# Second block: values token-major first, query/key jobs head by head with attention steps of other heads between their matmuls, output sums taken head by head

## The chip, the cores and the metric

One core of one Trainium2 chip runs the whole program. The metric is the device time in microseconds (us) of one execution, median of the runs.

## What is computed

A model of four layers on 512 tokens of 1024 features, all in float32. The change lies in the second layer (`layer` 1 in the code), whose mixer is differential attention. Of the reference, cut to that:

```
u = x * (1.0 + sc1) + sh1
q, k, v = split(u @ w_in, 3)            # 8 heads, of each two halves c of 64 query/key columns, 128 value columns
logits = einsum('bhcqd,bhckd->bhcqk', q * 64 ** -0.5, k) + bias[h]   # keys of later 64-token chunks masked
p = softmax(logits)
pdiff = p[:, :, 0] - lam_full * p[:, :, 1]
out = einsum('bhqk,bhkd->bhqd', pdiff, v)
out = rms_norm_of_each_head(out) * norm_g * (1.0 - lambda_init)
x = layer_norm(alpha * x + (1.0 + g1) * (out @ w_out))
```

Layer 0 (another mixer, and the same gated FFN with a causal convolution) runs before it; an FFN and two more layers follow. The scales, shifts and gates (sc1, sh1, g1, ...) come from a vector c times `w_ada`, 192 tiles in all.

## The kernel before

The activations are kept feature-major: a tile is 128 features by 512 tokens. A product with a weight matrix is a row of **jobs**. A job is one 128-column slice of the weights, all k tiles of it: SP loads 512 KB into `RAW` (two buffers, the load of job j waits for the splitting of job j-2), ACT rounds it to fp32r (`WH`, four slots, waits until PE is through with job j-4), POOL subtracts to get the rest (`WL`, L449), and PE makes three products for each k tile, `WH` by `Uh`, `WH` by `Ul`, `WL` by `Uh` (L1135, L1137 when the bank is part of `junk`), so 24 matmuls of 512 columns for a job of 8 k tiles. Four PSUM banks (0, 1, 4, 7) take the results in turn. Phases of jobs stand in `plan()`; every engine walks through them in this order, in program order.

Beside the jobs run the **ada tiles**: a phase with `ada=a` also has one tile of `w_ada` for each job, from number a on. SP loads it (512 KB), DVE multiplies it by `CB` and sums along the row (`ada_sum`, L1217). Tiles 96 and later need two such sums, for two vectors (L1213 into `junk`, L1214); these are the tiles of double width. In a phase, DVE does the ada tile of a job ahead of the job's epilogue.

Layer 0 ends with `down` of group 2: 8 jobs of only 6 k tiles, 18 matmuls each. Its epilogue is DVE's: `XT` plus bank times gate (L1319), and the running sum of `XT` in `ZS` (L1303) for the layer norm. The ada tiles are 104 to 115 in the phase before it, and none in this phase. The layer norm follows; its last part makes the 8 tiles of `Uh` and `Ul` one by one. POOL scales `XT` in the meantime (L436).

Layer 1's mixer then has these parts:
- `qkcopy`, 16 jobs: eight query tiles, then eight key tiles, copied by ACT to `QD`. Ada tiles 116 to 131.
- `v`, 8 jobs: each is copied to `TT`, transposed on PE by four matmuls (L1101), and copied to `VD` (token-major). Ada tiles 132 to 139.
- Attention in 32 **steps** (head h = it // 4, query tile b = it % 4, keys 0 to 128 (b + 1)). PE: `scores` (L965), two matmuls, one for each half c. DVE: `logits`, scale and bias out of PSUM (L1556), row maximum (L1561). ACT: `diff_exp` (L540). DVE: `diff`, reciprocal, scaling, difference of the two halves (L1571 to L1573) into `PD`. PE: `turn`, transposes of `PD` (L975). ACT: copy to `PTD` (L863). PE: `av`, by the values (L984). ACT: copy to `ON` and squares (L547, L548). PE runs scores two steps ahead of turn. No job runs in this part.
- After all steps: one root (L869), 32 scalings on DVE (L1588), and for each head four transposes (L916), DVE's scaling by `norm_g` (L1595), ACT's rounding to `OH` (L872), DVE's rest to `OL` (L1598).
- `res`, 8 jobs on `OH`, `OL`; then a layer norm.

Of the kernel before, what the change touches and what calls it, by code (L numbers as in the profile page):

```python
# [21 lines left out]
F32 = mybir.dt.float32  # L22
# [32 lines left out]
def plan():  # L55
# [75 lines left out]
def ada_width(a):  # L131

    return 2 if 96 <= a < 164 else 1
# [57 lines left out]
def build(nc, a, out):  # L191
    with ExitStack() as stack:
# [31 lines left out]
        Ul = at("Ul", [KT, TC], A_U + 24 * KB, F32R)  # L224
        ZS = at("ZS", [TC], A_U)
# [48 lines left out]
        DTMP = at("DTMP", [4 * DHD], A_Y + 5 * KB)  # L274
        ZD = at("ZD", [3, 2, T], A_U + 32 * KB)
        PD = at("PD", [2, T], A_U + 24 * KB)
        PTD = at("PTD", [2, T], A_U + 28 * KB)
# [37 lines left out]
        def banks_of(p):  # L315

            return (0, 1, 4, 7) if p["layer"] < 2 else (0, 1)

# [52 lines left out]
        D_J_END = next(p["j0"] for p in PHASES if first(p, "res", 1))  # L371
# [73 lines left out]
        def _(pool):  # L445
# [8 lines left out]

            def biases(p):
                if first(p, "res", 1):
                    for h in range(DH):

                        pool.wait_ge(S(f"strip_land{h % 2}"), 16 * (h // 2 + 1))
                        pool.memset(STRIP[0:64, h % 2, 448:512], MASKED).then_inc(S("strip_ready"), 1)  # L460
# [18 lines left out]
            for n, p in enumerate(phases):  # L479
                def body(i, p=p):  # L480
                    for u in range(4):
                        lo(i * 4 + (p["j0"] + u), u, u % 2)

# [59 lines left out]
        def diff_square(act, it):  # L543
            h, b = divmod(it, 4)
            act.wait_ge(S("d_av"), it + 1)
            at_least(act, S("d_sq"), it - 1)
            act.activation(ON[:, b, h * P:(h + 1) * P], BANK[6 + it % 2][:, 0:P], ACT.Copy)  # L547
            act.activation(TT[:, it % 2, 0:P], BANK[6 + it % 2][:, 0:P], ACT.Square,  # L548
                           accum_out=SS[:, 8 * b + h:8 * b + h + 1]).then_inc(S("d_sq"), 1)
# [86 lines left out]
        def _(act):  # L636
# [7 lines left out]

            def round_next(i, p, u):
# [21 lines left out]
            for t in range(KT):  # L667
                act.activation(Uh[:, t, 0:T], XT[:, t], ACT.Identity, bias=B2[:, t, 0:1], scale=G2[:, t, 0:1])
# [8 lines left out]
            def ln_act(p, idx):  # L677
# [12 lines left out]
                for t in range(KT):  # L690
# [5 lines left out]
                    else:  # L696
                        act.activation(Uh[:, t, 0:T], XT[:, t], ACT.Identity, bias=B2[:, t, 0:1], scale=G2[:, t, 0:1])
# [19 lines left out]
            def epilogue(i, p, u):  # L717
# [22 lines left out]
                elif kind == "qkcopy":  # L740
                    act.wait_ge(S("pe_job"), j + 1)
                    act.activation(flat(QD[:, ds(jl, 1)]), bank[:], ACT.Copy).then_inc(S("bank_read"), 1)
# [61 lines left out]
            for n, p in enumerate(phases):  # L804
                if p["kind"] in ("v", "gate_o", "qkcopy", "down", "ab", "na_q", "na_k", "na_v"):

                    act.wait_ge(S("bank_read"), p["j0"])
# [35 lines left out]
                if first(p, "res", 1):  # L843
                    act.wait_ge(S("d_begin"), 1)
                    act.dma_start(DLAM[:], a["dlam"]).then_inc(S("dlam_land"), 16)
                    for h in range(2):
                        load_strip(act, h)
                    act.wait_ge(S("lam_sums"), 1)
                    act.activation(SM[:, 2:4], SM[:, 0:2], ACT.Exp).then_inc(S("lam_exp"), 1)
                    diff_exp(act, 0)  # L850
                    for it in range(DH * 4):
                        h, b = divmod(it, 4)
                        n_keys = P * (b + 1)
                        if b == 0 and 1 <= h < DH - 1:

# [999 lines left out]
```

## Time and profile before

| | |
|---|---|
| median of 3 runs | 3207.25 us (3206.34 to 3211.78) |
| the profiled execution | span 3195.0 us from first to last instruction; its own device time is not recorded |
| PE busy | 2928.1 us, 92% of the span |
| DVE, ACT, POOL busy | 1597.5, 1129.9, 1092.2 us |
| chain that ended last | PE 75%, DVE 11%, issue 6%, ACT 4% |

The median of the runs stands 12.25 us above the profile's span. The busy time of PE is that of the whole program; what one part is worth is read from the stretch in which it runs.

### The profile page before, as it was taken

To read this page: it belongs to the slowest core of one execution; us is meant where nothing else is said; L and a number is where in the kernel's file an instruction comes from. 1 tells how busy PE (TensorE), PEld (TensorE's weight loads), DVE (VectorE), ACT (ScalarE), POOL (GpSimd) and SP (SyncE) were. 2 spreads that over 40 slices of the span, in tenths; PEclk is the share of its full clock that TensorE was granted. 3 is DMA by queue.
4 is the path that set the end of the run, shared out by engine and by line. 5 is a ranking of instruction groups with operands and counts; after the bars stand their busy time and mean duration, and the time that the engine had idled before them with its cause. 6 is when DMAs were issued, how large, how long until landed. Compare 5 with 4: busy or idle time off the path is not lost.

```text
span 3195.0 us, 39561 instructions
## 1 busy us (share of the span) xinstructions
PE 2928.1 (92%) x14050; PEld 2385.3 (75%) x14050; DVE 1597.5 (50%) x2324; ACT 1129.9 (35%) x1839; POOL 1092.2 (34%) x501
## 2 busy tenths in 40 slices
PE   4898899997987899999799799999979989989999
PEld 3675588885864677887586688888868878868887
DVE  6646786895678488946422421111241465531111
ACT  3233443334235343423411321221333347642222
POOL 2340444454520254444231132323213233234443
PEclk9999899998987899999899899999989989999999
DMA  5451255552530145544111121112112110022222
GB/s 227 144 191 53 106 197 189 186 204 79 197 124 17 60 145 184 191 138 138 35 66 53 40 66 61 65 66 66 60 40 73 53 48 21 24 79 95 97 99 86
DMA packets 90127, 324.36 MB, mean 102 GB/s; under 512 B 10004, under 2 KB 12820, under 8 KB 89496
## 3 DMA queue, kind: packets, MB, share of 16 engines
q1 hardware_dynamic: 85392, 312.21, 28.2%
q10 hardware_dynamic: 4616, 10.63, 1.0%
q8 instruction: 67, 1.10, 0.1%
q14 instruction: 52, 0.43, 0.0%
HBM read 320.70 MB, written 2.10 MB: 101 GB/s over the span
## 4 chain that ended last, share of the span: by engine, by line
PE 75%; DVE 11%; issue 6%; ACT 4%; POOL 2%; DMA 2%; DVEq 0%; ACTq 0%; SPq 0%; POOLq 0%
PE bank L1135 54%; PE junk L1137 9%; PE bank L1064 2%; PE bank L1051 1%; DMA ADA<-in_ast 1%; PE bank L1152 1%; PE bank L1043 1%; DVE ADA L1214 1%; POOL WL L449 1%; PE bank L1023 1%; DVE junk L1213 1%; DVE ADA L1217 1%; DVE TA L506 1%; DVE Hl L510 1%; PE junk L1043 1%
## 5 line engine op out<-in xcount | busy, mean ns | idle before, releaser
L449 POOL TENSOR_TENSOR WL<-RAW,WH 128x1024 fp32r<-128x1024 f32 x392 | 977.6, 2495 | 1790.0 <-ACT WH L655 1433.6
L1135 PE MATMUL bank<-Uh,WH 128*128 128x512 f32 x1984 | 798.8, 403 | 95.1 <-DVE Ul L1470 82.2
L1135 PE MATMUL bank<-Ul,WH 128*128 128x512 f32 x1984 | 784.6, 395 | 0.0
L1135 PE MATMUL bank<-Uh,WL 128*128 128x512 f32 x1984 | 783.5, 395 | 0.0
L1135 PEld LDWEIGHTS bank<-Uh,WH 128*128 128x128 f32 x1984 | 377.6, 190 | 205.4 <-issue 81.9
L655 ACT ACTIVATE WH<-RAW 128x1024 fp32r<-128x1024 f32 x324 | 340.9, 1052 | 386.8 <-PE junk L1137 192.0
L1135 PEld LDWEIGHTS bank<-Uh,WL 128*128 128x128 f32 x1984 | 378.6, 191 | 82.0
L1135 PEld LDWEIGHTS bank<-Ul,WH 128*128 128x128 f32 x1984 | 379.2, 191 | 78.1
L1135 PE MATMUL bank<-Hh,WH 128*128 128x512 f32 x864 | 340.8, 394 | 14.9 <-DVE Hl L510 14.9
L1135 PE MATMUL bank<-Hl,WH 128*128 128x512 f32 x864 | 339.5, 393 | 0.0
L1135 PE MATMUL bank<-Hh,WL 128*128 128x512 f32 x864 | 339.3, 393 | 0.0
L1319 DVE SCALAR_TENSOR_TENSOR XT<-bank,GATE,XT 128x512 f32 x112 | 84.0, 750 | 481.8 <-PE junk L1137 242.8
L1217 DVE CUSTOM_DVE_ANT_0 ADA<-ADA,CB 128x1024 f32<-128x1024 f32 x124 | 181.7, 1470 | 124.9 <-DMA ADA<-in_ast 115.3
L1135 PEld LDWEIGHTS bank<-Hh,WH 128*128 128x128 f32 x864 | 163.8, 190 | 53.7 <-DVE Hl L510 19.2
L1135 PEld LDWEIGHTS bank<-Hh,WL 128*128 128x128 f32 x864 | 163.7, 189 | 34.8
L1135 PEld LDWEIGHTS bank<-Hl,WH 128*128 128x128 f32 x864 | 163.8, 190 | 34.6
L1377 DVE SCALAR_TENSOR_TENSOR TT<-bank,TT 128x512 f32<-128x512 f32 x64 | 44.3, 692 | 278.1 <-ACT TT L763 173.2
L1137 PE MATMUL junk<-Ul,WH 128*128 128x256 f32 x512 | 144.1, 282 | 0.0
L1137 PE MATMUL junk<-Uh,WH 128*128 128x256 f32 x512 | 144.1, 281 | 0.0
L1137 PE MATMUL junk<-Uh,WL 128*128 128x256 f32 x512 | 143.7, 281 | 0.0
L1213 DVE CUSTOM_DVE_ANT_0 junk<-ADA,CB 128x1024 f32<-128x1024 f32 x68 | 100.0, 1470 | 58.4 <-DMA ADA<-in_ast 48.5
L1427 DVE RECIPROCAL NRS<-NRS 128x512 f32<-128x512 f32 (+1 forms) x16 | 66.4, 4153 | 121.6 <-ACT NRS L559 89.1
(288 smaller groups left out, 4310.0 us busy)
## 6 DMA issues: line engine op xcount, KB each, us to landing
RAW<-in_wst SPq DMA_DIRECT2D x392, 512.0 KB, 3.3
ADA<-in_ast SPq DMA_DIRECT2D x192, 512.0 KB, 4.5
NST<-in_nstrip ACTq DMA_DIRECT2D x16, 192.0 KB, 2.3
XT<-in_xt SPq DMA_DIRECT2D x1, 2048.0 KB, 15.3
STRIP<-in_strip ACTq DMA_DIRECT2D x8, 256.0 KB, 2.7
DX<-in_dx ACTq DMA_DIRECT2D x1, 2048.0 KB, 7.9
out_xt<-XT SPq DMA_DIRECT2D x1, 2048.0 KB, 6.2
CB<-in_cb ACTq DMA_DIRECT2D x2, 512.0 KB, 4.1
```

The costliest lines, as they stand in the source:

```text
L449: pool.tensor_tensor(WL[:, s4], RAW[:, s2], WH[:, s4].bitcast(F32), ALU.subtract)\
L506: dve.tensor_tensor(TA2[:, half], TA2[:, half], TG[:, half], ALU.mult).then_inc(S("ffn_prod"), 1)
L655: act.activation(WH[:, c % 4], RAW[:, c % 2], ACT.Copy).then_inc(S("hi_done"), 1)
L1043: mm = pe.matmul(BANK[bank][:, 0:256], w, x, start=m == 0, stop=m == 2)
L1064: mm = pe.matmul(BANK[6 + it % 2][:, 0:P], PTN[:, it % 2, s * P:(s + 1) * P], VN[:, tile, t * P:(t + 1) * P], start=s == 0, stop=s == 3)
L1135: mm = pe.matmul(bank_of(p, u)[:], w[:, u, k], x[:, k, 0:T], start=st and m == 0, stop=en and m == 2)
L1137: mm = pe.matmul(BANK[2 + u % 2][:, 0:C], w[:, u, k], x[:, k, T:TC], start=st and m == 0, stop=en and m == 2)
L1213: dve.tensor_tensor_reduce(JUNK[:], tile, CB[:, 0], 1.0, 0.0, ALU.mult, ALU.add, AD[:, u, 0:1])
L1217: dve.tensor_tensor_reduce(tile, tile, CB[:, 0], 1.0, 0.0, ALU.mult, ALU.add, AD[:, u, 0:1])\
L1319: ins = dve.scalar_tensor_tensor(out=flat(XT[:, ds(jl, 1)]), in0=bank[:], scalar=gate_of(jl), in1=flat(XT[:, ds(jl, 1)]), op0=ALU.mult, op ...
L1377: ins = dve.scalar_tensor_tensor(out=TT[:, u % 2, 0:T], in0=bank[:], scalar=0.0, in1=TT[:, u % 2, 0:T], op0=ALU.max, op1=ALU.mult)
L1427: link(dve.reciprocal(NRS[:, u % 2, 0:w], NRS[:, u % 2, 0:w]))
```

## The change

- `v` becomes `vt` and comes first: 8 jobs whose weights lie in another order (`wide_jobs`), so that a job holds 512 value columns of two k tiles. The activations (`U1h`, `U1l`, new names for `Uh`, `Ul` without the context columns) are the stationary side, the weights move, and the result is token-major in four banks for each half. The transposes and DVE's copies go; ACT copies four banks to `VD` after every fourth job.
- `qkcopy` becomes `qkd`: query and key tile of a head follow each other, and their jobs are cut in halves of 12 matmuls (`projection`). The attention steps of head h stand between the half jobs of head h + 1. Scores, turn and av have one bank or pair of banks each (4 and 5, 6, 7); turn lags scores by two steps, av by three.
- Head by head follow the root (`diff_root`, as Exp of -0.5 times Ln, with one Newton step in `head_norm`), the scalings, `turn_back`, `head_out`, `head_lo`.
- In place of the projections of a ninth head stand the first four `res` jobs, one k tile (12 matmuls) for each of the last steps (`residual`). The other four run afterwards as before.
- The 24 ada tiles of `qkcopy` and `v` move: the phase `qkd` has none, `down` of layer 0's last group has 8 (116 to 123, of double width), `vt` has 8, and the FFN of layer 1 has ada tiles also in its second `down`. The number of double sums goes from 68 to 64.

In the diff the three long loops are those of ACT, of PE and of DVE, in this order.

```diff
-    h = ffn(0, 8, 0, (56, 72, 80, 96, 104, None))
-    add("qkcopy", 16, 1, "u", 16, ada=116)
-    add("v", 8, 1, "u", 16, ada=132)
+    h = ffn(0, 8, 0, (56, 72, 80, 96, 104, 116))
+    add("vt", 8, 1, "u", 16, ada=124)
+    add("qkd", 16, 1, "u", 16)
     add("res", 8, 1, "o", 8, gate=2)
-    h = ffn(1, 24, h, (140, 156, 164, None, 180, None))
+    h = ffn(1, 24, h, (132, 148, 156, 172, 180, None))
...
+        VT_BANKS = ((0, 1, 4, 5), (6, 7, 0, 1))
+        D_BACK = (2, 3, 2, 3, 2, 3, 4, 5)
...
+            def diff_pool():
+                for n in range(3):
+                    lo(D_J0 + n, n, n % 2)
+                mask_strip(0)
+                mask_strip(1)
+                for t in range(DH):
+                    for j in (D_J0 + 2 * t + 3, D_J0 + 2 * t + 4):
+                        lo(j, j % 4, j % 2)
+                    if t >= 2:
+                        mask_strip(t)
...
+                for it in range(D_N + 5):
+                    t, b = it // 4 + 1, it % 4
+                    if b == 0 and t <= DH:
+                        copy_job(D_J0 + 2 * t - 1, QD[:, 8 + t - 1])
...
+                    if 1 <= it <= D_N:
+                        diff_exp(act, it - 1)
+                    if b == 0 and t <= DH:
+                        round_hi(D_J0 + 2 * t + 3, (2 * t + 3) % 4)
+                    if b == 2 and t < DH:
+                        copy_job(D_J0 + 2 * t, QD[:, t])
+                        round_hi(D_J0 + 2 * t + 4, (2 * t + 4) % 4)
+                    if 2 <= it < D_N + 2:
...
+                        act.activation(PTD[:, it % 2, 0:n_keys], BANK[6][:, 0:n_keys], ACT.Copy).then_inc(S("d_pt"), 1)
+                    if 3 <= it < D_N + 3:
+                        diff_square(act, it - 3)
+                        if (it - 3) % 4 == 3:
+                            diff_root(act, (it - 3) // 4, steps)
...
+                    if b == 0 and it >= 8:
+                        h = (it - 8) // 4
+                        act.wait_ge(S("d_out"), h + 1)
+                        act.activation(OH[:, h], TT[:, h % 2, 0:T], ACT.Copy).then_inc(S("o_hi"), 1)
+                for u in range(4):
+                    if u >= 1:
+                        round_hi(D_RES + 3 + u, (3 + u) % 4)
+                    epilogue(0, residual, u)
...
+            for it in range(D_N + 3):
+                t, b = it // 4 + 1, it % 4
+                if it < D_N - 4:
+                    projection(t, b)
+                else:
+                    residual(it - (D_N - 4), (0, 2, 1))
+                if b == 0 and it >= 8:
+                    turn_back((it - 8) // 4)
+                if it < D_N:
+                    scores(it)
+                if 2 <= it < D_N + 2:
+                    turn(it - 2)
+                if it >= 3:
+                    av(it - 3)
+                if it >= D_N - 4:
+                    residual(it - (D_N - 4), (3,))
+            turn_back(7)
+            residual(7, range(4))
...
+                for it in range(D_N + 6):
+                    if it % 4 == 1 and it >= 9:
+                        head_lo((it - 9) // 4)
+                    if it == 2:
+                        lambda_of()
+                    if 2 <= it < D_N + 2:
+                        diff(it - 2)
+                    if it % 4 == 0 and it >= 8:
+                        head_out((it - 8) // 4)
+                    if it < D_N:
+                        logits(it)
+                    if it % 4 == 3 and 7 <= it:
+                        head_norm((it - 7) // 4)
```

What this does to the order of instructions is shown at three places. The first is PE's, in the middle of the attention steps. Before (L965 scores, L975 turn, L984 av; `x3` is three instructions in a row):

```order
L965 MATMUL bank<-QD 128x128 x2
L975 MATMUL bank<-IDENT,PD 128x128 x3
L984 MATMUL bank<-VD,PTD 128x128 x2
L965 MATMUL junk<-QD 128x256 x2
L975 MATMUL bank<-IDENT,PD 128x128 x4
```

And of the change, at the start of a head (L1061 the last three of 12 matmuls of a half job, L1120 `turn_back`, L1087 scores, L1097 turn, L1106 av, then the first three of the next half job):

```order
L1061 MATMUL bank<-U1h,WH 128x512
L1061 MATMUL bank<-U1l,WH 128x512
L1061 MATMUL bank<-U1h,WL 128x512
L1120 MATMUL junk<-IDENT,OD 128x128 x4
L1087 MATMUL bank<-QD 128x128 x2
L1097 MATMUL bank<-IDENT,PD 128x128 x3
L1106 MATMUL bank<-VD,PTD 128x128 x2
L1061 MATMUL bank<-U1h,WH 128x512
L1061 MATMUL bank<-U1l,WH 128x512
```

Every step of attention now has 12 matmuls of a job ahead of its scores. The second place is DVE's, at the same spot of a head. Before, only logits (L1556, L1561) and diff (L1571 to L1573) alternate:

```order
L1572 TENSOR_SCALAR PD<-ZD,SM 128x256
L1573 SCALAR_TENSOR_TENSOR PD<-ZD,SM,PD 128x256
L1556 SCALAR_TENSOR_TENSOR ZD<-junk,STRIP 128x512 x2
L1561 TENSOR_REDUCE SM<-ZD 128x2
L1571 RECIPROCAL SM<-SM 128x2
```

Of the change (L1734 to L1739 `head_norm`, L1724 to L1726 diff, L1747 `head_out`):

```order
L1714 TENSOR_REDUCE SM<-ZD 128x2
L1734 TENSOR_SCALAR SS<-SS 128x4
L1735 TENSOR_TENSOR RSC<-RSC 128x4
L1736 SCALAR_TENSOR_TENSOR RSC<-RSC,SS 128x4
L1737 SCALAR_TENSOR_TENSOR RSC<-RSC 128x4
L1739 TENSOR_SCALAR OD<-OD,RSC 128x128 x4
L1724 RECIPROCAL SM<-SM 128x2
L1725 TENSOR_SCALAR PD<-ZD,SM 128x384
L1726 SCALAR_TENSOR_TENSOR PD<-ZD,SM,PD 128x384
L1747 TENSOR_SCALAR TT<-junk,SM 128x512
```

The eight instructions of `head_norm` moved in ahead of the diff for which PE's next turn waits. The third place is DVE's in `down` of layer 0's last group, one job. Before:

```order
L1319 SCALAR_TENSOR_TENSOR XT<-bank,GATE,XT 128x512
L1303 TENSOR_TENSOR ZS<-ZS,XT 128x512
L150 REGISTER_ALU
L1318 REGISTER_ALU
L1319 ISA
```

Of the change (L1365 and L1366 are the two sums of an ada tile, L1469 and L1453 the lines L1319 and L1303 of before):

```order
L1365 ISA junk,AD<-ADA,CB 128x1024
L1365 ISA AD 128x1
L1366 ISA ADA,AD<-ADA,CB 128x1024
L1366 ISA AD 128x1
L1468 REGISTER_ALU
L1469 ISA
L1469 SCALAR_TENSOR_TENSOR XT<-bank,GATE,XT 128x512
L1453 TENSOR_TENSOR ZS<-ZS,XT 128x512
```

Two sums over an ada tile now stand ahead of each of the 8 epilogues.

## Rows read from the trace of the kernel before

**Rows 1.** The page: span, and busy time of the engines.
```profile
span 3195.0 us, 39561 instructions
PE 2928.1 (92%) x14050; PEld 2385.3 (75%) x14050; DVE 1597.5 (50%) x2324; ACT 1129.9 (35%) x1839; POOL 1092.2 (34%) x501
```

**Rows 2.** Busy time by stretch, layer 1's mixer, and one of layer 0's.
```profile
core 0: us, PE busy (x) PEld busy (x) DVE busy (x) ACT busy (x) POOL busy (x), PEclk, DMA share, GB/s
266.00:310.00 44.00, 37.45 (x145) 25.10 (x144) 32.18 (x109) 14.40 (x46) 0.00 (x0) 1.00 0.00 1
...
785.80:797.50 11.70, 9.89 (x25) 5.70 (x26) 10.59 (x14) 10.46 (x14) 11.70 (x7) 0.75 0.00 0
797.50:884.50 87.00, 87.00 (x386) 72.02 (x385) 53.72 (x69) 25.22 (x32) 45.95 (x19) 1.00 0.56 193
884.50:929.80 45.30, 42.11 (x201) 34.51 (x199) 36.19 (x42) 11.42 (x15) 20.33 (x7) 1.00 0.53 175
929.80:1042.00 112.20, 79.07 (x368) 52.72 (x368) 88.43 (x197) 66.06 (x259) 1.16 (x8) 0.74 0.07 21
1042.00:1061.40 19.40, 12.59 (x50) 10.15 (x50) 16.99 (x49) 6.60 (x11) 0.00 (x0) 0.74 0.00 0
1061.40:1101.30 39.90, 39.84 (x174) 32.51 (x174) 13.72 (x17) 12.45 (x16) 21.73 (x8) 1.00 0.29 93
```

**Rows 3.** Waits, attention and what follows: total us, times, longest.
```profile
PEld bank L975 <- DVE PD L1573: 44.6, 26, 3.4
```

**Rows 4.** The chain: matmuls of jobs (start us, length us).
```profile
890.43 5.48 PE bank L1135 x24
896.35 5.47 PE bank L1135 x24
```

**Rows 5.** PE in order of time, one head's scores to the next's.
```profile
966.49 0.49 PE L965 MATMUL bank<-QD 64*128 64x128 f32 x4
969.59 0.90 PE L975 MATMUL bank<-IDENT,PD 128*128 128x128 f32 x3 [2.61 <-DVE PD L1573]
...
979.38 0.44 PE L975 MATMUL bank<-IDENT,PD 128*128 128x128 f32 x2 [0.94 <-DVE PD L1573]
979.97 0.49 PE L965 MATMUL bank<-QD 64*128 64x128 f32 x4
```

**Rows 6.** Groups of DVE after the steps: busy us, mean ns.
```profile
L1588 DVE TENSOR_SCALAR ON<-ON,RSC 128x128 f32<-128x128 f32 x32 | 6.4, 279 | 0.0
L1595 DVE TENSOR_SCALAR TT<-bank,SM 128x512 f32<-128x512 f32 x8 | 5.9, 749 | 0.6
L1598 DVE TENSOR_TENSOR OL<-TT,OH 128x512 fp32r<-128x512 f32 x7 | 4.8, 683 | 0.0
```

**Rows 7.** The page: POOL's splitting. Then DVE's lines L506 and L1295.
```profile
L449 POOL TENSOR_TENSOR WL<-RAW,WH 128x1024 fp32r<-128x1024 f32 x392 | 977.6, 2495 | 1790.0 <-ACT WH L655 1433.6
L506 DVE TENSOR_TENSOR TA<-TA,TG x44: 680/2208/2787, 414.4 to 1468.7; 128x512 f32<-128x512 f32 x44
L1295 DVE SCALAR_TENSOR_TENSOR TA<-bank,PRM,TA x88: 736/749/752, 399.0 to 1461.8; 128x511 f32<-128x511 f32 x44, 128x510 f32<-128x510 f32 x44
```

**Rows 8.** DVE in `down` of layer 0's group 1, with double ada tiles.
```profile
627.69 0.74 DVE L1319 SCALAR_TENSOR_TENSOR XT<-bank,GATE,XT 128x512 f32 x1
631.87 3.19 DVE L1213 CUSTOM_DVE_ANT_0 junk<-ADA,CB 128x1024 f32<-128x1024 f32 x1 [3.44 <-DMA ADA<-in_ast]
638.32 0.74 DVE L1319 SCALAR_TENSOR_TENSOR XT<-bank,GATE,XT 128x512 f32 x1
...
666.79 0.74 DVE L1319 SCALAR_TENSOR_TENSOR XT<-bank,GATE,XT 128x512 f32 x1
```

**Rows 9.** DVE in `down` of group 2: first and last epilogue of 8.
```profile
733.73 0.75 DVE L1319 SCALAR_TENSOR_TENSOR XT<-bank,GATE,XT 128x512 f32 x1 [1.08 <-PE bank L1135]
...
764.06 0.75 DVE L1319 SCALAR_TENSOR_TENSOR XT<-bank,GATE,XT 128x512 f32 x1 [2.60 <-PE bank L1135]
764.85 0.69 DVE L1303 TENSOR_TENSOR ZS<-ZS,XT 128x512 f32<-128x512 f32 x1
```

More of the change, by code:

```diff
@@ L315, in banks_of @@
         def banks_of(p):
+            if p["kind"] == "res" and p["layer"] == 1:
+                return (0, 1, 2, 3)
             return (0, 1, 4, 7) if p["layer"] < 2 else (0, 1)
+        VT_BANKS = ((0, 1, 4, 5), (6, 7, 0, 1))
+        D_BACK = (2, 3, 2, 3, 2, 3, 4, 5)
         def bank_of(p, u):
@@ L369, in norm_after @@
             return None
-        D_J_END = next(p["j0"] for p in PHASES if first(p, "res", 1))
+        D_J0 = next(p["j0"] for p in PHASES if p["kind"] == "qkd")
+        D_RES = D_J0 + 16
+        D_N = DH * 4
         F_J_END = next(p["j0"] for p in PHASES if first(p, "res2", 2))
@@ L482, in body @@
                         lo(i * 4 + (p["j0"] + u), u, u % 2)
+                if p["kind"] == "qkd":
+                    diff_pool()
+                if p["kind"] == "qkd" or first(p, "res", 1):
+                    before = p
+                    continue
                 for u in range(3):
@@ L739, in epilogue @@
                     act.activation(flat(OS[:, ds(jl, 1)]), bank[:], ACT.Sigmoid).then_inc(S("bank_read"), 1)
-                elif kind == "qkcopy":
-                    act.wait_ge(S("pe_job"), j + 1)
-                    act.activation(flat(QD[:, ds(jl, 1)]), bank[:], ACT.Copy).then_inc(S("bank_read"), 1)
+                elif kind == "vt":
+                    if u == 3:
+                        act.wait_ge(S("pe_job"), j + 1)
+                        for b in range(4):
+                            act.activation(VD[:, b, i * T:(i + 1) * T], BANK[VT_BANKS[i][b]][:], ACT.Copy).then_inc(S("bank_read"), 1)
                 elif kind == "up":
@@ L900, in _ @@
                     body(n_rounds - 1)
+                elif p["kind"] == "vt":
+                    body(0)
+                    body(1)
+                elif first(p, "res", 1):
+                    body(1)
                 else:
@@ L1173, in _ @@
                     mlstm_pe(pe)
-                if first(p, "res", 1):
+                if p["kind"] == "vt":
+                    values_pe(pe, p)
+                    continue
+                if p["kind"] == "qkd":
                     diff_pe(pe)
+                    continue
                 if first(p, "res2", 2):
@@ L1661, in _ @@
                     mlstm_dve()
-                if first(p, "res", 1):
-                    dve.wait_ge(S("v_out"), 16)
-                    dve.sem_inc(S("d_begin"), 1)
+                if p["kind"] == "qkd":
                     diff_dve()
+                    continue
                 if first(p, "v", 0):
@@ L1764, in layout @@
     ffn(0)
-    st += [jobs(i["d_w_in"][0], every, range(24)), jobs(i["d_w_out"][0], every, range(KT))]
+    d_in = i["d_w_in"][0]
+    st += [wide_jobs(d_in[:, 2 * D:]), jobs(d_in, every, [c for h in range(DH) for c in (h, DH + h)]),
+           jobs(i["d_w_out"][0], every, range(KT))]
     ffn(1)
```

271 lines of the change are left out of this document (162 added, 109 removed).

## The prediction

> **What bounds the kernel now.** I read the page first, then the busy time by stretch, then within the attention the waits and PE in order of time, and last the rows on DVE and POOL sharing. The page says that PE is busy 92% of a span of 3195.0 us [rows 1], so only what PE does not do, or does slowly, is to be had. The stretches show where that is in this layer [rows 2]. From the first matmul of `qkcopy` (785.8) to the last of `res` (1101.3) the mixer takes 315.5 us. In 797.5 to 884.5 PE is never idle: 16 jobs in 87.0 us are 5.44 us a job and 0.2266 us a matmul. In 929.8 to 1042.0, the 32 steps, PE is busy 79.07 of 112.2 us and its clock stands at 0.74 on average, so it goes to and fro between 1.2 and 2.4 GHz. DVE is busy 88.43 us there, ACT 66.06, POOL and the DMA queues almost nothing. The wait that recurs is PE's turn on DVE's diff, 44.6 us in 26 times [rows 3]. Within one head (966.49 to 979.97, 13.48 us) PE is idle 2.61 and 0.94 us [rows 5]. Then come 19.4 us of a serial end (one root, 32 scalings, transposes, `OH`, `OL`), PE again at 0.74. So 131.6 us pass without one matmul of a job, and this is the stretch that the change fills.
>
> **The change part by part.** I build the time of the new mixer from the same start.
>
> Values first. `vt` has 8 x 24 = 192 matmuls of 512 columns, as `v` had: 43.5 us. The four transposes of each job go; they made a job of `v` 5.92 us (start to start, [rows 4]) against 5.44. Each tile of `U` is now used for 12 matmuls in place of 3, so that PE does not wait for the tiles as `qkcopy` did in 785.8 to 797.5 (one job in 11.7 us). The clock there is 0.75 [rows 2], and I leave that in: 0.25 x 11.7 = 2.9 us. `vt` is 46.4 us. The first job of `qkd` needs a bank that ACT copies third of four after the last `vt` job; at up to 0.75 us for 128x512 (the nearest row is L1595, [rows 6]) that is a wait of 2 us.
>
> Projections of head 0: two jobs, 10.9 us, with nothing between them.
>
> The loop: 35 turns, each with 12 matmuls of a job (28 of projections, 7 of `res`): 35 x 12 x 0.2266 = 95.2 us. Between them PE's part of attention: it takes 13.48 - 2.61 - 0.94 = 9.9 us for each head at a clock of 0.74 to 0.75. If the clock is whole this is 0.75 x 9.9 = 7.4 us, and with `turn_back`, four transposes more, 7.8; eight heads are 62.4 us. I take the whole clock because the stretch 266 to 310, steps of layer 0's mixer, has PE busy 37.45 of 44 us, 85%, at 1.00 [rows 2], and the loop will have PE busier than that. A head in the loop is then 4 x 2.72 + 7.8 = 18.7 us of PE.
>
> DVE against it. Now 88.43 / 8 = 11.05 us of busy time a head. Added in the loop are per head four scalings of 0.28 (L1588), four small ones that I take at 0.2 each, `head_out` 0.75 (L1595) and `head_lo` 0.68 (L1598) [rows 6]: 3.4 us, in sum 14.4. That lies beside PE's 18.7. But POOL, idle in the steps of before, now splits two jobs a head, 2.5 us each [rows 7]. A DVE operation on two SBUF tensors waits for it: L506 takes 0.68 us at the least, 2.2 in the median and 2.79 at the most, while L1295, which reads PSUM, never takes over 0.752 [rows 7]. If each splitting stops DVE for its whole length the head costs DVE 14.4 + 5.0 = 19.4 us, if never 14.4. The Trainium skill (GPSIMD Engine Reference, Specifications) says that POOL's SBUF interfaces are shared with VectorE and contend with its instructions on two SBUF inputs or in a 2-port mode; the rows agree for two inputs, and by that rule the scalings of diff, one SBUF input, could be held too. That speaks against this change, since what it fills with jobs it also fills with splittings.
>
> Order counts more than sums. Of DVE's 11.05 us for the four steps of a head I estimate 2.4 for the logits of the longest step and 1.2 for the diff behind it; with `head_norm` (the eight operations above, 1.9) that is 5.5 us in a row, and PE reaches the turn behind it after about 2.72 + 1.5 = 4.2 us, a half job and a fifth of its 7.8; at the next step `head_lo` waits for ACT's `OH` and stands ahead of diff again. I take 1.75 us of waiting a head, 14 us in all, with bounds of nothing (PE sets the pace) and of 4.3 (DVE at 19.4 and its waits for ACT besides, 23 a head). The other steps have slack: scores go two steps ahead, and ACT with its 66.06 us, plus 32 us of copies and roundings, has 12 to 13 us of work in a head of 20.
>
> The end: the last head's squares, root, norm, transposes, `head_out`, `OH`, `OL` stay serial. From [rows 6], 1.1 + 0.75 + 0.68, with the like on ACT and four small operations, it is 6.5 us. Then 12 matmuls of `res`, 2.7. The weights of the fifth `res` job can only be rounded when the first four end, all at the same place: one rounding and a splitting of 2.5 less the 9 matmuls that run meanwhile, 3 us. Four jobs, 21.8.
>
> Sum: 46.4 + 2 + 10.9 + 95.2 + 62.4 + 14 + 6.5 + 2.7 + 3 + 21.8 = 264.9 us against 315.5: **50.6 us less**.
>
> The ada tiles. In `qkcopy` they cost nothing (PE never idle, 87.0 of 87.0), so that taking them away gives nothing there. Where they go it is otherwise. `down` of group 2 has its 8 epilogues between 733.73 and 764.06, one every 4.3 us [rows 9], paced by PE. With double tiles DVE was the slow one in `down` of group 1: epilogues at 638.32 to 666.79, six intervals of 4.75 us [rows 8]. That is 2.3 us of sums and 2.4 us of POOL's splitting, one after the other. Here `ZS` (two SBUF inputs, 0.69, [rows 9]) comes on top: 5.45 us. In group 1 the second epilogue came 10.6 us after the first (627.69 to 638.32), 3.44 of it for the second tile's DMA, queued on SP behind a weight load that waits for POOL [rows 8]; the same order holds here. First epilogue at about 737, second at 745 to 747, six more of 5.45: 778 to 780 in place of 764. The layer norm waits for the last one, and nothing covers it. I take **14 us more**; the bounds are 5 (DVE never held by POOL, 4.2 a job, and the DMA wait only) and 20 (all held and all late). In layer 1's FFN four double and twelve single tiles in place of 16 single ones in an `up`, and 8 single ones in a `down` that had none: jobs of 5.44 us cover 2.4 us of sums there, nothing.
>
> Net: 50.6 - 14 = 36.6 us. The profiled span of 3195.0 would be 3158.4; against the median of the runs, 3207.25, the time is **3170.6 us**.
>
> **The rivals.** The loop paced by DVE. For it: 14.4 + 5.0 us of DVE work beside PE's 18.7, and that half of the inputs of each diff come late by design. Against it: PSUM readers are not held, and two of four steps have slack. At 23 us a head instead of 20.45 it costs 20 us more: 3191.
>
> All goes well: PE paces the loop (waits of 4 us, not 14) and the ada tiles cost 6, because DVE slips its sums between the splittings. For it speaks that PE can be four banks ahead in `down`. 3152.6.
>
> PE's clock. The steps of before have it at 0.74 though PE is busy 70%. If the short waits of each step keep it going to and fro in the loop too, its 157.6 us of PE work last 157.6 / 0.70 = 225 us at a mean of 0.70, 53.5 more than 171.6: 3224, slower than before. From a mean of 0.735 downwards this decides for slower. Against it: 85% busy gave 1.00 in 266 to 310, and the loop's work is 92% of its time. The Trainium skill (TensorE: Matmul & The Clock Gate, HAM oscillation) tells of a loop whose waits throttle PE again on every k tile; by that rule the waits would have to be long, and those that I expect are 1 to 2 us.
>
> **How the numbers follow.** The forecast has 0.60, DVE's pace 0.18, the good case 0.15, the clock 0.07, of which 0.05 slower and 0.02 the same. Forecast, DVE's pace and the good case are all faster: 0.93. A range of 3148 to 3195 takes in these three with their bounds (the good case less 4, DVE's pace with an ada cost 4 higher) and leaves the clock out; with what I overlook that is 8 in 10. The likeliest case alone is 3157 to 3184. A measurement of this kernel tells about 0.2%, 6.4 us, from no change.
>
> **What would show it.** From the first matmul of `vt` to the last of `res` about 265 us. In the loop PE busy over 88% at a clock of 0.95 or more, a head every 20 to 21 us, and turn waiting for diff once or twice a head, after `head_norm`. In `down` of layer 0's last group epilogues 5.4 us apart, DVE sums of 2.4 to 3.4 us among them, and the layer norm 13 to 15 us later. I am wrong if epilogues stay at 4.1 us, if a head takes 23 us or more, or if the loop shows a clock of 0.8.

## The result and the profile after

| | before | after |
|---|---|---|
| median | 3206.8 us (3204.82 to 3211.78, 4 runs) | 3153.76 us (3149.35 to 3154.85, 4 runs) |
| profiled span | 3195.0 us | 3147.6 us (its run: 3149.35) |

The medians differ by 53.0 us, forecast 36.6 (3170.6 us). The ratio is 0.9849, 95% interval 0.9828 to 0.987; it is not the quotient of the two medians, and by it the change is 48 us faster (42 to 55). The two profiled spans differ by 47.4. Run twice more on other chips beside the kernel before, the change gave 3165.13 against 3204.61 (0.9886, 0.9863 to 0.991) and 3160.95 against 3196.68 us (0.9883, 0.9864 to 0.9901): 39.5 and 35.7 us by the medians, 36.5 and 37.4 by the ratios. What of the 53 us belongs to the change has to be read from the trace.

The page, then busy time by stretch, which answers to [rows 1, 2]: `vt`, the loop's middle, the last steps, `res`.

```profile
span 3147.6 us, 39276 instructions
PE 2890.3 (92%) x14018; PEld 2354.1 (75%) x14018; DVE 1610.0 (51%) x2339; ACT 1131.4 (36%) x1854; POOL 1085.5 (34%) x501
```

```profile
core 0: us, PE busy (x) PEld busy (x) DVE busy (x) ACT busy (x) POOL busy (x), PEclk, DMA share, GB/s
801.80:847.20 45.40, 45.40 (x192) 37.02 (x190) 35.20 (x36) 19.09 (x24) 34.88 (x16) 0.95 0.43 150
...
862.00:1000.00 138.00, 130.25 (x671) 93.19 (x670) 96.10 (x231) 82.77 (x267) 36.72 (x21) 0.99 0.21 67
1000.00:1036.00 36.00, 29.54 (x144) 21.77 (x143) 17.70 (x47) 11.33 (x42) 0.00 (x0) 0.93 0.04 15
1036.00:1063.70 27.70, 26.93 (x108) 21.23 (x106) 21.95 (x15) 11.46 (x15) 19.68 (x7) 0.90 0.35 114
```

In the loop PE is busy 130.25 of 138 us, 94%, at a clock of 0.99, where the steps of before had 79.07 of 112.2 at 0.74 [rows 2]. Its last part is not so: in 1000 to 1036 the clock is 0.93, and around the start of that stretch the granted clock is 0.50, half speed (1.2 GHz):

```profile
999.00:1003.00 4.00, 3.92 (x9) 3.14 (x10) 2.06 (x4) 1.08 (x5) 0.00 (x0) 0.50 0.37 131
```

The busy shares on the page are as before: the gain is seen only by stretch.

The chain, from which the parts of the mixer are measured (start us, us): all of `vt`; the longest scores (L1087) of heads 3 to 5 with logits (L1709, L1714) behind them; the last k tile of the first `res` jobs; the wait for `WL`; the last four `res` jobs.

```profile
801.09 46.12 PE bank L1046 x192
848.95 13.88 PE bank L1061 x60
...
931.27 1.08 PE bank L1087 x4
932.38 1.30 DVE ZD L1709 x2
933.70 1.22 DVE SM L1714
...
950.94 1.08 PE bank L1087 x4
...
970.61 1.08 PE bank L1087 x4
...
1038.78 2.78 POOL WL L463
1041.60 11.17 PE bank L1280 x48
1052.78 10.89 PE junk L1280 x48
```

From 801.09 to 1063.67 the mixer takes 262.6 us, forecast 264.9, before 315.5. A head takes 19.67 us (931.27, 950.94, 970.61), forecast 20.45; the last such interval (990.23 to 1013.71), with the clock at half in it, is 23.5. In each head the chain leaves PE once, for 5.4 us of DVE's work in a row: the logits of the longest step and their maximum, shown above, and behind them `head_norm` and the diff, up to 937.75. The waits in that stretch, of PE's weight loads (PEld) and of its matmuls (the last line is of the same view drawn out to 1064):

```profile
PEld bank L1097 <- DVE PD L1726: 7.1, 16, 1.0
PE junk L1120 <- DVE OD L1739: 5.8, 6, 1.4
PE bank L1120 <- DVE OD L1739: 3.1, 2, 2.2
PE bank L1076 <- DVE OL L1752: 2.2, 1, 2.2
PE bank L1097 <- DVE PD L1726: 2.1, 8, 0.6
PE junk L1076 <- issue: 0.8, 1, 0.8
PE bank L1280 <- POOL WL L463: 0.7, 1, 0.7
```

The 44.6 us of turn on diff [rows 3] are waits of the weight loads, and those are 7.1 now. PE's matmuls themselves waited there for 29.3 us in 19 times before, and for 2.1 now. In their place stands `turn_back` (L1120) waiting for the scaled head.

DVE in `down` of layer 0's group 2, answering to [rows 9]:

```profile
738.91 0.74 DVE L1469 SCALAR_TENSOR_TENSOR XT<-bank,GATE,XT 128x512 f32 x1
...
741.78 3.41 DVE L1366 CUSTOM_DVE_ANT_0 ADA<-ADA,CB 128x1024 f32<-128x1024 f32 x1
745.12 0.74 DVE L1469 SCALAR_TENSOR_TENSOR XT<-bank,GATE,XT 128x512 f32 x1
745.90 2.12 DVE L1453 TENSOR_TENSOR ZS<-ZS,XT 128x512 f32<-128x512 f32 x1
...
752.77 0.74 DVE L1469 SCALAR_TENSOR_TENSOR XT<-bank,GATE,XT 128x512 f32 x1
...
778.67 0.75 DVE L1469 SCALAR_TENSOR_TENSOR XT<-bank,GATE,XT 128x512 f32 x1
...
783.03 4.87 DVE L1603 TENSOR_TENSOR XT<-XT,bank 128x512 f32<-128x512 f32 x8 [1.36 <-PE bank L1290]
```

The last epilogue is at 778.67 in place of 764.06. A sum that takes 1.22 us when POOL is idle takes 3.41 here, `ZS` 2.12 in place of 0.69. The same centring of the layer norm stood at 767.05 before:

```profile
767.05 4.87 DVE L1457 TENSOR_TENSOR XT<-XT,bank 128x512 f32<-128x512 f32 x8 [0.41 <-PE bank L1145]
```

So the layer norm begins 16.0 us later, and the mixer's first matmul 15.3 (801.09 against 785.8). Mixer and delay make 52.9 - 15.3 = 37.6 us. Of the other 9.8 of the spans' 47.4, 3.5 lie between the end of `res` and the layer norm behind layer 1's FFN (its centring at 1464.00 against 1505.12). The change moves ada tiles there, but values_first (experiment 2), which moves none there, has 3.3 of these us too, so that nothing points to the tiles. The last 6.3 lie in layers 2 and 3, which the change doesn't touch; the last section tells of such differences.

Where two traces differ already ahead of `down`, the delay is best counted from the clearing of `ZS` by DVE (MEMSET), just ahead of it. From there to the centring it is 35.1 us before (731.96 to 767.05) and 51.0 in the change (732.02 to 783.03): 15.9 us more. In all seven traces that have the double sums and the whole splitting here it is 50.7 to 51.2.

### The profile page after: what moved, and what is told of

Read it like the earlier page. It is cut to its first block, busy times and chain, and to the rows that moved or that the text cites. A ratio compares the mean times of both kernels' runs of the same rounds, so it can differ in the third digit from the quotient of the medians.

```text
span 3147.6 us, 39276 instructions
## 1 busy us (share of the span) xinstructions
PE 2890.3 (92%) x14018; PEld 2354.1 (75%) x14018; DVE 1610.0 (51%) x2339; ACT 1131.4 (36%) x1854; POOL 1085.5 (34%) x501
## 4 chain that ended last, share of the span: by engine, by line
PE 75%; DVE 11%; issue 6%; ACT 4%; POOL 2%; DMA 1%; DVEq 0%; ACTq 0%; SPq 0%; POOLq 0%
PE bank L1280 49%; PE junk L1282 9%; PE bank L1061 2%; PE bank L1208 2%; PE bank L1046 1%; DVE ADA L1366 1%; POOL WL L463 1%; PE bank L1195 1%; DMA ADA<-in_ast 1%; PE bank L1187 1%; PE bank L1167 1%; PE bank L1297 1%; DVE junk L1365 1%; DVE ADA L1369 1%; PE junk L1187 1%
## 5 line engine op out<-in xcount | busy, mean ns | idle before, releaser
L1280 PE MATMUL bank<-U1h,WH 128*128 128x512 f32 x960 | 380.1, 396 | 30.4 <-DVE U1l L1617 19.1
L1280 PE MATMUL bank<-Uh,WH 128*128 128x512 f32 x832 | 340.1, 409 | 55.6 <-DVE Ul L1619 55.0
L1280 PE MATMUL bank<-U1l,WH 128*128 128x512 f32 x960 | 377.1, 393 | 0.0
L1280 PE MATMUL bank<-U1h,WL 128*128 128x512 f32 x960 | 376.8, 393 | 0.0
L1280 PE MATMUL bank<-Hh,WH 128*128 128x512 f32 x864 | 340.4, 394 | 15.8 <-DVE Hl L545 15.8
L1280 PE MATMUL bank<-Ul,WH 128*128 128x512 f32 x832 | 330.6, 397 | 0.0
L1280 PE MATMUL bank<-Uh,WL 128*128 128x512 f32 x832 | 330.2, 397 | 0.0
L1469 DVE SCALAR_TENSOR_TENSOR XT<-bank,GATE,XT 128x512 f32 x112 | 83.9, 750 | 426.6 <-PE junk L1282 241.5
L1280 PEld LDWEIGHTS bank<-Uh,WH 128*128 128x128 f32 x832 | 158.6, 191 | 106.6 <-issue 45.5
L1280 PEld LDWEIGHTS bank<-U1h,WL 128*128 128x128 f32 x960 | 182.3, 190 | 38.5
L1280 PEld LDWEIGHTS bank<-U1l,WH 128*128 128x128 f32 x960 | 182.4, 190 | 37.1
L1280 PEld LDWEIGHTS bank<-Uh,WL 128*128 128x128 f32 x832 | 159.2, 191 | 35.0
## 6 DMA issues: line engine op xcount, KB each, us to landing
XT<-in_xt SPq DMA_DIRECT2D x1, 2048.0 KB, 15.5
```

The source lines that it names most:

```text
L1280: mm = pe.matmul(bank_of(p, u)[:], w[:, u, k], x[:, k, 0:T], start=st and m == 0, stop=en and m == 2)
L1469: ins = dve.scalar_tensor_tensor(out=flat(XT[:, ds(jl, 1)]), in0=bank[:], scalar=gate_of(jl), in1=flat(XT[:, ds(jl, 1)]), op0=ALU.mult, op ...
```

## The experiments

**1. Only the ada tiles moved** (ada_move), the kernel before with

```
-    h = ffn(0, 8, 0, (56, 72, 80, 96, 104, None))
-    add("qkcopy", 16, 1, "u", 16, ada=116)
-    add("v", 8, 1, "u", 16, ada=132)
+    h = ffn(0, 8, 0, (56, 72, 80, 96, 104, 116))
+    add("qkcopy", 16, 1, "u", 16)
+    add("v", 8, 1, "u", 16, ada=124)
...
```

> The kernel before with only the move of the ada tiles: eight double tiles in down of layer 0's second group, none in qkcopy, layer 1's tiles as in the change. Theory (the move costs, DVE and POOL share a port in down, nothing covers the layer norm behind it): the last epilogue about 14 us later and the layer norm's first centring 14 to 16 us later; the attention and the rest as before; the time 14 to 16 us longer, about 3222. Rival (the moved sums lie in slack and the 16 us seen in the trace of the change come from something else): within 2 us of before. In qkcopy and v no gain in either case.

Measured: 3213.22 against 3195.5 us, ratio 1.0049 (1.003 to 1.0068), 15.7 us by the ratio. The price is real, and it is the place's. The line `ZS` in `down`, all eight of them (duration min/median/max in ns, first and last start), in this kernel and in the one before:

```profile
L1303 DVE TENSOR_TENSOR ZS<-ZS,XT x8: 691/1366/2482, 742.8 to 782.5; 128x512 f32<-128x512 f32 x8
```

```profile
L1303 DVE TENSOR_TENSOR ZS<-ZS,XT x8: 691/692/695, 734.5 to 764.8; 128x512 f32<-128x512 f32 x8
```

39.7 us from first to last against 30.3, and the first comes later besides. The centring stands at 786.08, 50.9 us behind the clearing of `ZS` (735.14) against 35.1 before: 15.8 us more, the same as in the change and as in the time.

**2. Only the values first** (values_first): in the kernel before, `vt` and then `qkcopy`, nothing interleaved.

```
-    add("qkcopy", 16, 1, "u", 16, ada=116)
-    add("v", 8, 1, "u", 16, ada=132)
+    add("vt", 8, 1, "u", 16, ada=116)
+    add("qkcopy", 16, 1, "u", 16, ada=124)
...
```

> The kernel before with values first (token-major, before the query and key jobs) and nothing interleaved; the ada tiles stay in the mixer (8 beside the values, 16 beside the query and key jobs). Theory: the four transposes of each of eight jobs are gone (8 x 0.48 = 3.8 us), the wait for the tiles of U at the start is spread over 12 matmuls a tile (6.3 less 2.9 = 3.4 us), a wait of up to 2 us for a bank and 1 to 2 us for the last double sum ahead of the scores: 3 to 6 us shorter than before. What the change gains beyond this is the interleaving's. Rival (the values' order is where the gain comes from, the steps between jobs bring little): 15 us or more shorter.

Measured: 3193.89 against 3195.5, ratio 0.9985 (0.997 to 1.0), 4.8 us by the ratio, just at the edge of what can be told. In the trace, from the layer norm's first centring (771.27) to the end of `res` (1101.26), it takes 330.0 us against 334.3 before and 280.6 after. So of the 53.6 us between the last two 4.3 come from the values, and by difference 49.3 from the rest of the change, the interleaving with the output sums taken head by head; these two were not run apart. The steps are as slow as they were:

```profile
929.00:1042.00 113.00, 79.56 (x368) 53.12 (x368) 88.50 (x198) 66.09 (x259) 1.17 (x8) 0.74 0.08 22
```

**3. Single tiles in `down`** (ada_single): the change with tiles 184 to 191, one sum each, in place of 116 to 123.

```
+def ada_tile(a):
+    return a if a < 116 else 184 if a == 116 else a - 8
...
```

> The change, with the same number of ada tiles beside down of layer 0's second group, but single tiles (1.2 us of sums each in place of 2.4; the numbers are those of the last eight tiles, so that later stretches take four more double tiles in an up of layer 1). Theory (what delays the layer norm is that double sums, the splitting and ZS do not fit in one job of 4.1 us on DVE): epilogues follow PE at 4.1 to 4.3 us, the layer norm begins 0 to 3 us after that of the kernel before in place of 16, and the time is 12 to 15 us shorter than the change. Rival (any ada tile there delays, through the queue of the weights or POOL's port): 8 us or more of the delay stay, gain below 8 us.

Measured: 3146.61 against 3195.5, ratio 0.9835 (0.9813 to 0.9856). The centring stands at 773.35, 9.7 us ahead of the change's 783.03, and 40.7 us behind the clearing of `ZS`. Neither expectation on it holds: 5.6 of the 15.9 us stay with half the sums. The change did not run beside it, so the time says no more.

```profile
L1458 DVE TENSOR_TENSOR ZS<-ZS,XT x8: 691/2094/2504, 737.0 to 769.9; 128x512 f32<-128x512 f32 x8
```

`ZS` takes 2.1 us in the median. DVE also waits 2.4 us for the DMA of two tiles, against 0.3 in the change. What delays is not the sums' own length alone.

**4. POOL's splitting cut short** (short_splits_2): the change with one k tile of each job split in place of all, in `down` of layer 0's group 2, `vt` and `qkd` (`short[0]`). It leaves out seven eighths of the weights' low parts there, so its output is not the reference's.

```
+                n = 1 if short[0] else KT
-                pool.tensor_tensor(WL[:, s4], RAW[:, s2], WH[:, s4].bitcast(F32), ALU.subtract)\
+                pool.tensor_tensor(WL[:, s4, 0:n], RAW[:, s2, 0:n], WH[:, s4, 0:n].bitcast(F32), ALU.subtract)\
```

> The change with POOL's splitting cut to one eighth of each weight job (first k tile only) in down of layer 0's second group, in the values and in the attention loop. It leaves out seven eighths of the low parts of the weights there, so the output is not the reference's. Theory (DVE's operations on two SBUF tensors are held for as long as POOL splits): in down the sums and ZS take their shortest times, 2.4 and 0.7 us, epilogues stand 4.0 to 4.3 us apart and the last one 8 to 12 us earlier than in the change (770 or before); in the loop little changes (0.5 us a head at most), since PE's wait there comes from the order of DVE's work. Rival (DVE's own sums and the wait for the tile's DMA pace down): the last epilogue within 3 us of 779.

Measured, in two runs: 3135.18 against 3204.61, ratio 0.9792 (0.9764 to 0.9819).

```profile
L1457 DVE TENSOR_TENSOR ZS<-ZS,XT x8: 691/693/885, 736.3 to 767.1; 128x512 f32<-128x512 f32 x8
```

With all double sums in place, the eight stand in 30.8 us again. The centring comes at 770.22, 38.1 us behind the clearing of `ZS`, so that 12.9 of the 15.9 us are gone and 3.0 stay. Shorter splittings also free `RAW` earlier for the queue that loads the tiles, but that is not where the gain lies: DVE waited 0.3 us for tiles in the change and waits 1.7 here. So it is the hold by POOL that makes the delay, but for 3.0 us: of DVE's 2.4 us of sums, 0.7 of epilogue and 0.7 of `ZS` a job PE's 4.1 cover all, as long as POOL does not stop two of them. In the loop's middle a head keeps its 19.7 us, with the same waits of 5.8 and 1.0 us: what POOL holds there costs nothing, and the rival of DVE's pace falls. The last interval is 21.3 us in place of 23.5; the clock is at half in it for a shorter time, and why is not shown.

The change beside it had 3165.13 us, 30 more, which is more than `down` explains. The two traces (after_2 and this one) differ by 29.1 us: 15.2 up to the centring (12.8 of it in `down`), 3.4 in the mixer, and 10.5 in layers 2 and 3, whose splittings are whole in both (last section).

**5. The tiles in the loop** (ada_loop_2): none in `down`, eight single ones in the loop, where DVE waits for scores.

```
+    add("qkd", 16, 1, "u", 16, ada=124, ada_n=8)
...
                         diff(it - 2)
+                    if it % 4 == 2 and it < D_N:
+                        ada_job(it // 16, 124, it // 4 % 4)
```

> The change, with no ada tile beside down of layer 0's second group; eight single tiles (the last eight numbers) go into the attention loop instead, one a head, between DVE's diff and logits of the third step, where DVE waits about 2.5 us for scores; the values have tiles 116 to 123, and four more double tiles stand in an up of layer 1. Theory (the 16 us are the price of the place, DVE in the loop has room: it is busy 70% of the time there): the layer norm begins within 1 us of the kernel before, 15 us earlier than in the change, a head in the loop stays at 19.7 us or takes up to 0.5 more; 11 to 16 us shorter than the change. Rival (held by POOL's splitting a sum of 1.2 takes 3.4, the order of DVE's work delays the turns): a head 21 us or more, gain below 6 us.

Measured: 3151.33 against 3204.61, ratio 0.9842 (0.9823 to 0.986). The change beside it had 3165.13: 13.8 us less. In `down`:

```profile
L1464 DVE TENSOR_TENSOR ZS<-ZS,XT x8: 691/692/694, 737.1 to 767.9; 128x512 f32<-128x512 f32 x8
```

The centring is at 770.12, 35.6 us behind the clearing of `ZS`, as before. A head stays at 19.7 us with DVE busy 103.19 of 135 us. The theory holds: the 24 tiles need not cost anything that these traces show.

**6. The norm and `turn_back` one step later, together** (norm_later)

```
-                    if it % 4 == 3 and 7 <= it:
-                        head_norm((it - 7) // 4)
+                    for h in range(DH):
+                        if it == 4 * h + 7 + SH(h):
+                            head_norm(h)
...
```

`SH` is 1 for heads 0 to 4; `turn_back`, `OH` and `OL` move by it too.

> The change, with the norm of each of the first five heads, its turning back and the pair OH/OL one step later, so that the norm does not stand ahead of the longest step's diff. Theory (the 1.03 us that PE waits for each head are due to the order of DVE's work, 0.88 of it to turn_back waiting for the scaled head): the waits of five heads go or halve, 2 to 5 us shorter than the change. Rival (DVE has no slack in the loop, so that the wait only moves to another step): within 1 us of the change, with the same 1 us a head of idle PE at another matmul.

Measured: 3161.58 against 3195.5, ratio 0.9889 (0.9865 to 0.9913), no better than the change in either later comparison (0.9886, 0.9883). PE, one head:

```profile
901.73 0.65 PE L1121 MATMUL junk<-IDENT,OD 128*128 128x128 f32 x4 [0.91 <-DVE OD L1741]
903.17 0.66 PE L1098 MATMUL bank<-IDENT,PD 128*128 128x128 f32 x4 [0.15 <-DVE PD L1728]
```

The same wait, 1.06 us, at the same two matmuls, one step on; a head takes 19.9 us. Both had moved, so this could not tell why.

**7. Only `turn_back` later** (edges_2), and the last four copies of the values in the order 2, 3, 0, 1.

```
-                if b == 0 and it >= 8:
-                    turn_back((it - 8) // 4)
+                for h in range(7):
+                    if it == 4 * h + 8 + SH(h):
+                        turn_back(h)
...
+                        for b in ((2, 3, 0, 1) if i else range(4)):
```

> The change with turn_back, OH and OL of heads 0 to 4 one step later while the norm stays where it is (in norm_later both moved and the wait stayed), and with ACT's last four copies of the values in the order in which the first query job wants the banks. Theory: of the 1.03 us that PE waits in each head 0.88 is turn_back for the scaled head, that wait goes in five heads (0.2 us a head left in the turns), and the 1.76 us before the first query job fall to 0.2 to 0.5: 5 to 6 us shorter than the change. Rival (DVE's order sets the step, the wait moves to the turn): 1 us a head stays, only the 1.5 us at the start go.

Measured: 3166.21 against 3204.61, ratio 0.9891 (0.9869 to 0.9914), and 3165.13 for the change beside it: no gain. The wait at the first query job is 0.78 in place of 1.74 us, a little more than expected. The loop does the opposite of my theory:

```profile
847.20 0.47 PE L1062 MATMUL bank<-U1h,WH 128*128 128x512 f32 x1 [0.78 <-ACT VD L842]
...
896.64 0.55 PE L1098 MATMUL bank<-IDENT,PD 128*128 128x128 f32 x3 [1.68 <-DVE PD L1728]
...
897.41 0.78 PE L1062 MATMUL bank<-U1h,WH 128*128 128x512 f32 x1
...
918.36 0.55 PE L1098 MATMUL bank<-IDENT,PD 128*128 128x128 f32 x3 [1.69 <-DVE PD L1728]
```

The turn waits now, for the diff behind the norm, and longer: 8.4 us in five times in the loop's middle. `turn_back` with its wait had only stood ahead of it. A head takes 20.1 us, and two of them 21.7, in which the clock fell.

**8. The norm behind the diff** (norm_behind_2): the kernel of experiment 7, and for heads 0 to 4

```
                         diff(it - 2)
+                    for h in range(5):
+                        if it == 4 * h + 8:
+                            head_norm(h)
```

> The kernel edges with the norm of heads 0 to 4 behind the next step's diff in place of ahead of it; turn_back, OH and OL stay one step later, and the copies of the values stay in the new order. In edges PE waited 1.69 us a head in one piece, at the turn behind the norm, and the clock fell to half after some of them. Theory (PE's wait in each head is the diff that stands behind the longest logits and the norm; the norm's 1.9 us are what it is short of): the wait goes, idle 0.2 us a head or less in the loop's middle, two jobs in 18.9 us or less in place of 19.7; 0.78 us at the first query job stay as in edges; 4 to 6 us shorter than the change. Rival (the longest logits alone are enough, or the scaled head comes late again): 0.7 us a head or more stay, at the turn or at turn_back.

Measured: 3151.01 against 3196.68, ratio 0.9862 (0.9841 to 0.9883), the change beside it 3160.95: 9.9 us less by the medians. The two intervals overlap, so that the trace has to decide. PE's longest scores in two heads, and the stretch:

```profile
891.64 1.13 PE L1088 MATMUL bank<-QD 64*128 64x512 f32 x4
910.36 1.13 PE L1088 MATMUL bank<-QD 64*128 64x512 f32 x4
```

```profile
862.00:1000.00 138.00, 133.98 (x700) 96.94 (x700) 104.59 (x239) 84.07 (x274) 36.70 (x21) 1.00 0.23 72
```

18.7 us a head, PE 97% busy: the matmuls alone, 4 x 2.72 + 7.8. The turn's waits for the diff fall from 8.4 to 0.2 us against experiment 7, by this one edit. The order was the wait. (The norm behind the diff without the later `turn_back` was not run.) The mixer takes 254.5 us in this trace (802.24 to 1056.77), 7.9 less than in the change beside it.

**9. Both** (best_2), the kernels of 5 and 8 together.

> ada_loop and norm_behind together: no ada tile in down of layer 0's second group, eight single ones in the loop, the norm behind the diff. If the two are independent: layer norm 15 us and the loop 4 to 6 us shorter than in the change, 17 to 20 us in all, ratio to before about 0.980. Rival (the single sums take the room that the norm needs, 3.4 us when POOL holds them): the loop's idle time is back at 1 us a head and the time is that of ada_loop.

Measured: 3145.46 against 3196.68, ratio 0.9831 (0.9812 to 0.985), 15.5 us less than the change beside it; the two profiled spans, 3143.4 and 3163.9, differ by 20.5. The forecast was 17 to 20: the medians fall a little short of it, the spans reach it. Its mixer takes 256.1 us (785.73 to 1041.79) and starts 15.8 us earlier. Of the versions that compute everything it has the lowest ratio, 0.9831, but ada_single with 0.9835 can't be told from it. One of its middle heads takes 19.03 us (912.99 to 932.02), the others 18.7. The single sum ahead of it took its 1.22 us and was not held; what got in the way was the small addition behind every fourth tile (`ada_out`), 128x4, which takes 0.17 us alone and 2.22 beside a splitting (909.12 to 911.59). The turn behind it waits 0.50 us.

```profile
909.38 2.22 DVE L1394 TENSOR_TENSOR MOD<-AD,PRM 128x4 f32<-128x4 f32 x1
...
912.99 1.13 PE L1099 MATMUL bank<-QD 64*128 64x512 f32 x4
932.02 1.13 PE L1099 MATMUL bank<-QD 64*128 64x512 f32 x4
```

**10. The change again** (after_2 and after_4), as the measure beside the others; times above.

> The change once more, on the chip of the three runs beside it, as their measure. Jobs of the fourier and neighbourhood layers took 8.32 us in some profiled runs and 8.48 in others with PE never idle at a clock of 1.00 (ada_move and ada_single against the two kernels); over the 64 jobs and more this is 10 us. Expected: times in two groups some 10 us apart, whatever the kernel, and 1.4 to 1.6% shorter than before.

> The change once more, on the chip of the two runs beside it, as their measure: 1.1 to 1.6% shorter than before. Its own traces should show the same 19.7 us a head and 16 us at the layer norm whichever of the two durations (8.32 or 8.48 us) the later layers' jobs have.

Both traces have the mixer of the first: `vt` to the end of `res` in 262.4 us, layer norm at 785.38 and 783.80, 50.9 and 51.2 us behind the clearing of `ZS`. The two groups of times that I expected can't be told in four runs (3162 to 3170, 3157 to 3166), and the first of them is 1.1% shorter than before, not the 1.4 to 1.6% that I expected.

## Why the prediction was right

In the order of its sum, forecast then trace. The parts are cut at the chain's pieces above.

- `vt` 46.4: 46.1. The slow clock at its start, 2.9 us taken from `qkcopy`, is there (0.95 over 45.4 us, so about 2.3).
- Bank wait 2: 1.74 (848.95 less 801.09 + 46.12). Another order of the copies brought it down to 0.78 (experiment 7), so it is ACT's copies.
- Projections 10.9: 11.1 (48 of the 60 matmuls in 13.88).
- Jobs 95.2, attention 62.4, waits 14, in sum 171.6: 169.3 from there to 1029.36, where the last av ends. In the middle heads PE's share is right to a tenth of a microsecond, as experiment 8 shows with the waits gone. The waits were 9.6 us in place of 14 (the rows of waits, without the last 2.2 of `turn_back`, 2.2 of OL and 0.7 of WL), 1.03 a head in the middle in place of 1.75:

```profile
916.84 0.66 PE L1120 MATMUL junk<-IDENT,OD 128*128 128x128 f32 x4 [0.87 <-DVE OD L1739]
918.09 0.55 PE L1097 MATMUL bank<-IDENT,PD 128*128 128x128 f32 x3 [0.17 <-DVE PD L1726]
```

The mechanism, the norm ahead of the diff, was named, and my 5.5 less 4.2 us for DVE and PE would have given 1.3. **The size was off** by the second wait that I added, behind `head_lo`: in the middle heads it is not there, and it comes once, near the end (0.56 us at 1024.62). The remaining 2.1 us (169.3 less 157.6 and 9.6) the sum had at nothing: after waits of 1.45 and 0.16 us the clock stood at half from about 997 to 1004, and 12 matmuls of `res` took 5.2 us (from 999.08) in place of 2.9 (from 1010.77).
- Serial end 6.5: 6.0.
- `residual(7)` 2.7: 5.5. **This term failed**: I had put the whole clock, and it is at half after the two waits of 2.2 us (0.50 in 1035 to 1041).

```profile
1028.55 1.05 PE L1106 MATMUL bank<-VD,PTD 128*128 128x128 f32 x8
...
1032.50 0.66 PE L1120 MATMUL bank<-IDENT,OD 128*128 128x128 f32 x4 [2.20 <-DVE OD L1739]
1035.39 0.80 PE L1076 MATMUL bank<-OH,WH 128*128 128x512 f32 x1 [2.23 <-DVE OL L1752]
```

- Wait for `WL` 3: 0.73. Together with the term ahead of it 6.2 against 5.7. The two errors look like one, since slower matmuls hide more of the splitting; that is argued, not tried.
- Four jobs 21.8: 22.1.

The sum is 2.3 us off, and partly by luck: the waits were 4.4 us too many, and the half clock at two places, which the sum had not, gave 4.9 back.

One reading of the prediction was wrong without harm: the 44.6 us of turn on diff are waits of the weight loads. PE's matmuls left 33.1 of the 112.2 us of the steps idle and waited 29.3 for the diff; no term was worked out from the 44.6.

The **ada move** was put at 14 with bounds of 5 and 20; it is 15.3 to 16.0. Double sums, the splitting and `ZS` did add up, as named, in 39.8 us from the first epilogue to the last, 5.7 an interval where I had 5.45. They are not even: 6.2 and 7.7 us (738.91, 745.12, 752.77), since a sum and `ZS` can both be held in one job, and 3.9 for the last one, when POOL has no more to split. The Trainium skill (GPSIMD Engine Reference, Specifications) says that POOL contends with VectorE's instructions on two SBUF inputs or in a 2-port mode; experiment 4 agrees for two inputs (`ZS` 693 ns in the median with short splittings against 1367), and a scaling with one SBUF input is held too at times, below.

Net, 37.6 us by the trace and 36.6 forecast; the mixer was 2.3 us better than forecast and the ada move 1.3 worse. Against the first comparison's 53 the forecast is 17 us short, against its ratio 12. No term of the change accounts for those: 9.8 us of the spans' difference lie elsewhere, and the two other comparisons gave 36 to 40, or 0.9886 and 0.9883, where the forecast is 0.9886. I made the sum against one profile and took it from a median 12.25 us above that profile. In every run whose span is known the time is 1.7 to 2.2 us above the span, so some 10 of the 12.25 are the difference between that execution and the others; which duration a run gets is worth that much.

Of the rivals, DVE's pace is refuted (experiment 4), the good case was right on the loop's order only with another order of DVE's work (experiment 8), and the clock did not go to and fro in the loop: 0.99 from 862 to 1000. The forecast took it that waits of 1 to 2 us leave the clock whole. In the middle heads the waits are below 0.9 us and it stayed whole; behind the wait of 1.45 us in the last interval, and behind the two of 2.2 us at the end, it was at half, and after a single wait of 1.7 us it is at times (experiment 7).

## What to carry to other kernels

Fill a stretch of short dependent steps with matmuls of another stage, and then look at the order of the vector engine's work within a step: the one result that the matmul engine needs next goes first, and work of a finished unit behind it. Moving the waiting consumer alone only moves the wait. Work that is to be hidden belongs where its engine waits for others, and not in the last phase ahead of a serial stage, where another engine's use of SBUF can hold it.

## What the hardware did unexpectedly

Two traces of one program differ in the duration of jobs with PE never idle and the clock at 1.00. The change in its first profile and in a later one (after_2), 120 us of the later layers:

```profile
1920.00:2040.00 120.00, 120.00 (x694) 105.81 (x693) 22.70 (x36) 27.71 (x38) 35.12 (x15) 1.00 0.19 64
```

```profile
1920.00:2040.00 120.00, 120.00 (x681) 104.14 (x680) 22.71 (x36) 27.73 (x38) 34.07 (x15) 1.00 0.19 62
```

694 against 681 matmuls, 1.9%, or 8.32 and 8.48 us a job; over the 64 or so of such jobs this is an estimated 10 us in a run. The whole stretch from the last layer norm of layer 1 to the end lasts 1683.6 us in the first trace of the change and 1697.9 and 1699.6 in the later two, 14 to 16 us more. The traces with 694 or 695 matmuls in this window, that of before among them, lie at 1683.6 to 1690.8, those with 681 or 682 at 1697.9 to 1700.2. What decides it stays open.

A wait of 1.7 us in one piece put PE's clock to half for about 3 us in two of five heads (the first matmul of the half job behind 896.64 takes 0.78 in place of 0.48) and not in the others (918.36), with the same wait; the two waits of 0.87 and 0.17 us in the middle heads never did. In the last interval waits of 1.44, 0.17 and 1.27 us left the clock at 1.00 in norm_behind_2, while 1.45, 0.16 and 1.27 were followed by half the clock in best_2 (22.8 us for that interval against 21.2). So the waits alone do not tell it.

DVE's scaling of one SBUF tensor, 128x512, which took 0.547 us in the mean before, took up to 1.59 us while POOL was splitting (norm_behind_2):

```profile
917.87 1.59 DVE L1727 TENSOR_SCALAR PD<-ZD,SM 128x512 f32<-128x512 f32 x1
```
